# The experts' second weights move from the sync engine's DMA queue to ScalarE's

## What is computed

```
hid = xb @ w1[e] + b1[e]                      # w1[e]: 1024 x 2048, 8 MiB
glu = minimum(hid[:, :1024], 7.0)
lin = clip(hid[:, 1024:], -7.0, 7.0)
act = glu * sigmoid(1.702 * glu) * (lin + 1.0)
y   = (act @ w2[e] + b2[e]) * gate            # w2[e]: 1024 x 1024, 4 MiB
```

## Time and profile before

| | |
|---|---|
| median of 3 runs | 2637.34 us |
| profiled execution, its own time | 2637.1 us |
| its span, first to last instruction | 2635.1 us |
| mean granted TensorE clock | 0.969 |
| TensorE busy | 2499.3 us, 95% |
| VectorE / ScalarE / GpSimd busy | 39% / 15% / 7% |
| mean DMA rate over the span | 211 GB/s |

### The profile page before, as it was taken

One profiled execution on the slowest core, in us unless ns is written; L12 is line 12 of the kernel. 1 busy time (PEld: TensorE's weight loads), 2 busy tenths in 40 slices (PEclk: granted clock), 3 DMA queues, 4 the chain that ended last, 5 costly groups with the idle time before them and its releaser, 6 DMA issues.

```text
span 2635.1 us, 49056 instructions
## 1 busy us (share of the span) xinstructions
PE 2499.3 (95%) x20546; PEld 1392.9 (53%) x20546; DVE 1017.1 (39%) x2008; ACT 405.9 (15%) x797; POOL 195.1 (7%) x256
## 2 busy tenths in 40 slices
PE   5999989796999999999999999699999998999999
PEld 2444787653344433333344434345556544888888
DVE  5563655414333333333333333523145222455551
ACT  2411134412000000000000000101234201111100
POOL 0000000000111111111111111400000000000000
PEclk9999999887999999999999999799999999999999
DMA  7432000106999999999999999740200112222221
GB/s 275 156 128 96 2 3 1 67 0 248 413 422 422 421 422 422 421 422 422 422 422 422 422 422 384 253 164 33 96 33 33 32 32 64 64 96 64 88 66 54
DMA packets 143742, 555.43 MB, mean 211 GB/s; under 512 B 15760, under 2 KB 51632, under 8 KB 94240
## 3 DMA queue, kind: packets, MB, share of 16 engines
q1 hardware_dynamic: 127088, 515.22, 49.2%
q0 software_dynamic: 13984, 36.49, 3.8%
q10 hardware_dynamic: 2576, 2.36, 0.3%
HBM read 537.25 MB, written 16.78 MB: 210 GB/s over the span
## 4 chain that ended last, share of the span: by engine, by line
PE 92%; DVE 3%; ACT 2%; DMA 2%; issue 1%; POOL 1%; SPq 0%; POOLq 0%; DVEq 0%; ACTq 0%
PE psum L2501 25%; PE psum L2090 20%; PE psum L2517 13%; PE psum L2787 10%; PE psum L2816 5%; PE psum L2250 2%; PE psum L2706 2%; PE psum L2422 2%; PE psum L2683 1%; DMA ring<-in_ada_w 1%; PE psum L2364 1%; PE psum L2661 1%; PE psum L2390 1%; PE psum L2671 1%; PE psum L2078 1%
## 5 line engine op out<-in xcount | busy, mean ns | idle before, releaser
L2501 PE MATMUL psum<-ring,arena 128*32 128x512 f32 x6144 | 667.8, 594 | 10.2 <-DVE arena L1688 6.8
L2501 PEld LDWEIGHTS psum<-ring,arena 128*32 128x32 f32 x6144 | 196.8, 110 | 453.0 <-issue 452.3
L2090 PE MATMUL psum<-hT,ring 128*128 128x512 f32 x752 | 340.6, 610 | 3.5 <-ACT hT L833 3.5
L2517 PE MATMUL psum<-ring,arena 128*32 128x256 f32 x6144 | 338.3, 379 | 2.2 <-DVE arena L1722 2.1
L2517 PEld LDWEIGHTS psum<-ring,arena 128*32 128x32 f32 x6144 | 201.2, 110 | 146.5 <-issue 21.9
L2090 PEld LDWEIGHTS psum<-hT,ring 128*128 128x128 f32 x752 | 144.9, 196 | 182.2 <-issue 180.3
L1688 DVE STREAM_TRANSPOSE arena<-arena 128x768 f32<-128x768 f32 x33 | 32.3, 979 | 512.6 <-PE psum L2501 512.6
L764 POOL DMA_INDIRECT arena<-h_rows,small x102 | 99.9, 980 | 1294.8 <-issue 680.7
L2787 PE MATMUL psum<-ring 128*128 128x256 f32 x704 | 159.1, 379 | 0.5 <-ACT arena L819 0.5
L1017 ACT ACTIVATE arena<-arena 128x768 f32<-128x768 f32 x32 | 27.0, 843 | 823.3 <-DVE arena L1708 823.3
L2787 PEld LDWEIGHTS psum<-ring 128*128 128x128 f32 x704 | 133.7, 190 | 19.0 <-ACT arena L819 0.9
(11 more groups left out here) (393 smaller groups left out, 2553.3 us busy)
## 6 DMA issues: line engine op xcount, KB each, us to landing
ring<-in_exp_w SPq DMA_DIRECT2D x384, 1024.0 KB, 15.8
ring<-in_w_in SPq DMA_DIRECT2D x15, 2048.0 KB, 8.3
ring<-in_ada_w SPq DMA_DIRECT2D x12, 2048.0 KB, 7.8
ring<-in_w_ffn_in SPq DMA_DIRECT2D x22, 1024.0 KB, 7.7
expert_rows<-arena POOLq DMA_DIRECT2D x128, 96.0 KB, 6.0
ring<-in_w_ffn_out SPq DMA_DIRECT2D x8, 1408.0 KB, 6.8
ring<-in_w_out SPq DMA_DIRECT2D x2, 2048.0 KB, 7.9
ring<-in_w_o SPq DMA_DIRECT2D x2, 2048.0 KB, 8.5
```

Of the source, the lines that this page charges most:

```text
L2090: ins = mm(dst, l, r, start=(i == 0), stop=(i == len(parts) - 1))
L2501: ins = mm(bank[s][q * SG:(q + 1) * SG, :], XG[:, k, s * SG:(s + 1) * SG], w[:, q], start=(k == 0), stop=(k == KD - 1))
L2517: ins = mm(bank[3 + s // 2][q * SG:(q + 1) * SG, (s % 2) * 256:(s % 2 + 1) * 256], aT2k[:, s, k // 2, k % 2, :], w2_slot(k)[:, q * 256:(q ...
```

## The change

SP no longer issues `load_w2`; its queue holds the first weights only (and after the experts all that it held before). ScalarE issues `load_w2(j, e)` of the same expert e whose sigmoid it has just done, behind `load_b1(e + 1)`, for expert 0 too. The four loads wait for `w2_free` as before, now on ScalarE. The first increment of `w2_free` moves there as well. VectorE, TensorE and GpSimd are as they were.

```diff
@@ block.sync
-            w2_d = a["exp_w2"][0].rearrange("e (q p c) n -> e q p (c n)", p=P, c=2)
             sp.wait_ge(filled, plan.at["wo", KD - 1] + 1)
             sp.sem_inc(w1_free, QT4 * KD)
-            sp.sem_inc(w2_free, QT4 * KD)
...
-            def load_w2(it, e):
-                for q in range(QT4):
-                    sp.wait_ge(w2_free, it * (QT4 * KD) + QT4 * (2 * q + 2))
-                    sp.dma_start(w2_pair(q), w2_d[bass.ds(e, 1), q].rearrange("o p n -> p (o n)")).then_inc(w2_in[q], 16)
             load_w1(0, 0)
-            sp.wait_ge(rows_in, 16 * GROUPS)
-            load_w2(0, 0)
             sp.wait_ge(lin_ready, 1)
...
             with sp.Fori(0, last - 1) as i:
                 load_w1(i + 2, (i + 2) % EXPERTS)
-                load_w2(i + 1, (i + 1) % EXPERTS)
-            load_w2(last, EXPERTS - 1)
@@ block.scalar
+            w2_d = a["exp_w2"][0].rearrange("e (q p c) n -> e q p (c n)", p=P, c=2)
+
+            def load_w2(j, e):
+                for q in range(QT4):
+                    act.wait_ge(w2_free, (j * EXPERTS + e) * (QT4 * KD) + QT4 * (2 * q + 2))
+                    act.dma_start(w2_pair(q), w2_d[bass.ds(e, 1), q].rearrange("o p n -> p (o n)")).then_inc(w2_in[q], 16)
+            act.wait_ge(filled, plan.at["wo", KD - 1] + 1)
+            act.sem_inc(w2_free, QT4 * KD)
             with act.Fori(0, passes) as j:
                 load_b1(0)
                 with act.Fori(0, EXPERTS - 1) as e:
                     expert(j, e)
                     act.wait_ge(lin_ready, j * EXPERTS + (e + 2))
                     load_b1(e + 1)
+                    load_w2(j, e)
                 expert(j, EXPERTS - 1)
+                load_w2(j, EXPERTS - 1)
```

## The result

The changed kernel takes 2650.53 us (median of 6 runs, 2648.01 to 2651.21) against 2636.82 for the one before (6 runs): a ratio of 1.0046, 95% interval 1.0036 to 1.0056, so 9 to 15 us slower. Forecast: 2649.1 and +0.45%. The profiled execution's span went from 2635.1 to 2648.4 us, 13.3 us more; the experts account for 13.0 of them.

What follows compares the result with a forecast made beforehand. TensorE bounds the experts, with the DMA overdrawn. Slot 7's landing, 24.3 + 6.5 + 9.4 = 40.2 us, exceeds 28.4 of room by 11.8: 2637.1 + 11.8 = 2648.9, as a median 2649.1 us; range 2637 to 2662.

Steps and rivals of the forecast that it cites:

- The bound: In the experts' stage TensorE sets the pace at 31.29 us an expert; once loads stall it, the DMA does, at 31.87.
- The growth: In the experts' stage, first-weight loads land later by 0.576 us with each expert, because the DMA is overdrawn.
- both rivals on the rate: Weight loads through two queues: DMA moves more per second (2637 to 2645, chance 0.18) or less (2658 and above, 0.10).
- The room: From issue of an expert's last first-weight load (slot 7) to its use in hidden: 28.4 us, 24.3 used at the end.
- The onset: Stalls on slot 7's first weights begin 8.5 experts after expert 2, near 970 us.
- The late first load: Expert 0's second weights move from an idle DMA stretch into the overdrawn one: 6.5 us added backlog, bounds 5 and 9.9.
- The sharing: Two queues take turns, so second weights overtake slot 7's first weights, wanted sooner: 9.4 us later landing, bounds 0 and 9.9.
- ScalarE's issues: Four more load issues an expert on ScalarE, behind sigmoid and bias, fit its free time of over 20 us: cost 0.
- The signs that it named: Profile after: q10 traffic, landings, period, L2501 waits, 422 GB/s, idle stretches, and sigmoid 2.8 us after hidden, as listed beforehand.

Runs made afterwards that it cites:

- the first experiment: The changed kernel, but the sync engine issues expert 0's second weights early, where the kernel before does: 2645.86 us, ratio 1.0028.
- holding back: The changed kernel, but ScalarE holds second-weight pair q until slot 3 + q of the next expert's first weights has landed: 2646.48 us, ratio 1.0038.
- the stronger form: The changed kernel, but second-weight pairs 0 to 3 wait until the next expert's first-weight slots 5, 6, 7, 7 have landed: 2650.85 us, ratio 1.0049.

## Why the prediction was right

*The bound.* TensorE sets the pace until the backlog reaches the room, then the DMA does: shown by the chain, by the quarter megabyte less (stall 0) and more (15.9 us).

*The growth, 0.576 us an expert.* The period in the stalled stretch is 31.81 us against 31.29: 0.52 for the average over hidden(10) to hidden(31), 0.58 forecast. Where the queues alone are at work, from hidden(20) to the end, the first experiment lost 6.3 us in 11 to 12 experts, 0.52 to 0.57 each. The DMA rate did not change with two queues, 422 GB/s; both rivals on the rate are out.

*The room, 28.4 us.* The loads that TensorE waited for had 28.5 to 29.6 us from issue to landing, stall included.

*The onset,* forecast near 970 us: hidden(10), from 955.43, takes 0.1 us longer than those before it, and hidden(11) waits for slot 7 until 1005.46, about 0.5 us.

*The late first load, 6.5 us (bounds 5 and 9.9).* With one queue: 1.0 + 28.4 - 24.3 = 5.1 us, at the lower bound. Slots 1 to 3 landed after 13.5 us (median) in expert 3 instead of 8.5, 5.0 us more, and after 27.5 instead of 24.3 in expert 31, 3.2 more. So this term was 1.4 us or more too large. Why the difference shrinks is open. That the gathers used part of the idle time, as the lower bound supposed, fits, and was not tested.

*The sharing, 9.4 us (bounds 0 and 9.9).* With the first load early: 6.3 + 28.4 - 24.3 = 10.4 us, above the upper bound by 0.5. Two things may make up the excess, neither measured apart: besides the 9.9 us of second weights, gathers and stores take turns too; and the 24.3 us, read as slot 7's landing, are those of slots 1 to 3, while in the run with the late first load, where the trace has slot 7, it landed 1 us after them (28.5 against 27.5 in expert 31). The same would make the late first load's term smaller still. The term of the sharing also isn't a constant, as the run with a quarter of a megabyte less shows; it held because the queue was full where it counted. Equal turns were shown by the packets, 436 to 434. The errors of the two terms nearly cancel: 15.5 against 15.9 forecast, and that is luck.

*ScalarE's issues, 0.* In the expert at 1295 us the second weights were issued from 7.1 us after `hidden` ended (1302.16), forecast 6.8, and its sigmoid still starts 2.8 us after `hidden`'s end (1295.08 to 1297.86).

*The signs that it named.* Seen: q10 with the second weights, the period, waits at L2501 and never at L2517, the rate, the idle stretches, ScalarE's sigmoid, and about 28 us for slot 7. Missed: a first weight's landing of 25 us or more in 1287 to 1318, which should have risen from 19.4. It is 19.4 again:

```profile
ring<-in_exp_w SPq DMA_DIRECT2D x7, 1024.0 KB, 19.4
```

This median holds only slots 0 to 4, and the one before only slots 1 to 3, so neither holds slot 7. The prediction took it for all first weights, and expected in it a delay that mainly the late slots have. A small misreading beside it: slice 10 of the earlier trace rows has 413 GB/s, not 421 or 422; nothing rests on it.

*Not foreseen:* 1.7 us for hidden(1), which isn't of the change as far as the runs show (last section). Without it the forecast of 11.8 us stands against 11.3 measured in the stall.

*Left open:* why holding back gave 3.7 us where 5 to 9 were expected, and 13.7 us of stall in the stronger form where 7.4 was. The waits and chains show which load was late, not each packet's order.

## What to carry to other kernels

Where DMA and TensorE are both full, read how the landing time of one kind of load changes from the first iteration to the last, and set it against the time from issue to use: here a growth of 0.58 us an expert and 4.1 us of room left decided everything, and neither shows in a busy share. Look first which loads such a median holds: here it left out the one slot that stalled. In this stretch the second queue added no bandwidth; it only gave up the order of use, and loads that were wanted later overtook those wanted sooner. Expert 0's second weights could run in an idle stretch ahead of a full one, and issued there they took nothing from it.

## What the runs showed of the hardware

With two hardware queues full of 1 MiB loads the engines moved 436 packets of one and 434 of the other in 16 us, at 421 GB/s in total; over the slices of the stage it was 422, with one queue and with two.

TensorE's granted clock at hidden(1) fell to half for some 3 us in five of the nine profiles and not in the others. Windows 672 to 677 us, PEclk behind the busy times, first the changed kernel:

```profile
672.00:677.00 5.00, 4.89 (x32) 1.47 (x36) 4.86 (x14) 0.00 (x0) 0.26 (x1) 0.66 0.43 136
```

and the one with held-back pairs, which loads the same there:

```profile
672.00:677.00 5.00, 5.00 (x52) 1.63 (x48) 4.86 (x17) 0.00 (x0) 0.75 (x1) 1.00 0.41 116
```

Ahead of it TensorE had been idle for 3.4 us (before, 668.34 to 671.76; changed, 668.7 to 672.11). It fell with the DMA full (early first load: PEclk 0.72, DMA share 1.01) and with the DMA at 0.43, and stayed up in both cases too (before: 1.00 and 1.01; held back: 1.00 and 0.41), so the runs tie it to no part of the change. It costs 1.7 us where it comes: hidden(1) took 22.50 us in each of the five, against 20.81. What makes it come is open, and so is its part in the scatter between executions.
